# Twenty-four projections turned to 512-column token form, rounded blocks of the norms written from PSUM, and one weight split moved, in a three-block model on one core

## The reference

```python
def sqrelu_mlp(x, w1, w2):
    return jnp.square(jax.nn.relu(x @ w1)) @ w2
...
        x = layer_norm(ALPHA * x + mix, ln1_g[i], ln1_b[i])
        x = layer_norm(ALPHA * x + sqrelu_mlp(x, mlp_w1[i], mlp_w2[i]), ln2_g[i], ln2_b[i])
```

```python
    proj = jnp.einsum("bld,dp->blp", x, w_in)
    qkv, z, a, b, uv, gate_dn, gate_sgu = jnp.split(proj, offsets, axis=-1)
    qkv = jax.nn.silu(causal_depthwise_conv(qkv, conv_w)).astype(f32)
...
    y_dn = jnp.einsum("blc,cd->bld", o.reshape(bsz, seq, DN_DIM).astype(x.dtype), w_dn_out)
    y_sgu = spatial_gating(uv, sgu_ln_g, sgu_ln_b, spatial_w, spatial_b, w_sgu_out)
    y = jax.nn.sigmoid(gate_dn) * y_dn + jax.nn.sigmoid(gate_sgu) * y_sgu
    return jnp.einsum("bld,de->ble", y, w_out)
```

## Time and profile before

| | |
|---|---|
| median of 3 runs | 1267.28 us |
| profiled execution, its own time | 1265.15 us |
| its span | 1263.4 us |
| TensorE busy (matmul) | 1239.5 us, 98% |
| VectorE busy | 806.1 us, 64% |
| ScalarE busy | 607.2 us, 48% |
| mean granted TensorE clock | 0.999 of full speed |
| bytes moved | 205.00 MB, 162 GB/s |

### The profile page before, as it was taken

One profiled execution on the slowest core, in us unless ns is written; L12 is line 12 of the kernel. 1 busy time (PEld: TensorE's weight loads), 2 busy tenths in 40 slices (PEclk: granted clock), 3 DMA queues, 4 the chain that ended last, 5 costly groups with the idle time before them and its releaser, 6 DMA issues.

```text
span 1263.4 us, 20462 instructions
## 1 busy us (share of the span) xinstructions
PE 1239.5 (98%) x8838; PEld 1154.6 (91%) x8838; DVE 806.1 (64%) x946; ACT 607.2 (48%) x702; POOL 164.3 (13%) x137
## 2 busy tenths in 40 slices
PE   8999999999999999999999999999999999999997
PEld 8978999998999899999889999999998999999996
DVE  6477855657655875565888338833777775555556
ACT  4565434345636534434476457645734633333332
POOL 8400400001400040000401300040000050000000
PEclk9999999999999999999999999999999999999999
DMA  9814665553742475557665335672754465555550
GB/s 264 194 34 133 198 236 178 189 200 103 231 151 84 165 237 197 176 192 163 138 138 130 101 101 134 133 102 68 250 190 144 167 216 184 185 183 195 175 197 34
DMA packets 148219, 205.00 MB, mean 162 GB/s; under 512 B 13603, under 2 KB 117778, under 8 KB 148130
## 3 DMA queue, kind: packets, MB, share of 16 engines
q1 hardware_dynamic: 145906, 195.80, 52.1%
q0 software_dynamic: 2224, 7.90, 2.0%
HBM read 202.63 MB, written 1.05 MB: 161 GB/s over the span
## 4 chain that ended last, share of the span: by engine, by line
PE 83%; DVE 7%; DMA 4%; ACT 3%; SPq 2%; issue 1%; DVEq 0%; ACTq 0%
PE PS L385 37%; PE PS L390 18%; PE PS L513 8%; PE PS L456 2%; DMA ring<-in_w_in 2%; DVE w_lo L1158 2%; PE PS L993 2%; PE PS L1006 1%; ACT w_hi L1753 1%; PE PS L394 1%; SPq L2327 1%; PE PS L395 1%; PE PS L396 1%; DMA ring<-in_a_w_out 1%; PE PS L919 1%
## 5 line engine op out<-in xcount | busy, mean ns | idle before, releaser
L1158 DVE TENSOR_TENSOR w_lo<-ring,w_hi 128x2048 fp32r<-128x2048 f32 x182 | 429.9, 2367 | 208.0 <-ACT w_hi L1753 208.0
L1753 ACT ACTIVATE w_hi<-ring 128x2048 fp32r<-128x2048 f32 x182 | 347.7, 1912 | 246.8 <-PE PS L390 225.3
L385 PE MATMUL PS<-x_hi,w_hi 128*128 128x256 f32 x1168 | 284.1, 284 | 0.2 <-DVE x_lo L1650 0.2
L385 PE MATMUL PS<-x_lo,w_hi 128*128 128x256 f32 x1168 | 283.5, 283 | 0.0
L385 PEld LDWEIGHTS PS<-x_hi,w_hi 128*128 128x128 f32 x1168 | 223.7, 192 | 3.3 <-issue 1.5
L385 PEld LDWEIGHTS PS<-x_lo,w_hi 128*128 128x128 f32 x1168 | 224.0, 192 | 1.7
L1765 ACT ACTIVATE AR<-PS 128x512 f32<-128x512 f32 x154 | 87.2, 598 | 271.0 <-PE PS L390 176.9
L390 PE MATMUL PS<-x_hi,w_lo 128*128 128x256 f32 x1184 | 154.4, 283 | 0.2 <-DVE w_lo L1283 0.2
L385 PE MATMUL PS<-w_hi,o_hi 128*128 128x512 f32 x384 | 150.2, 391 | 0.8 <-DVE o_lo L1407 0.8
L385 PE MATMUL PS<-w_hi,o_lo 128*128 128x512 f32 x384 | 150.0, 391 | 0.0
L390 PEld LDWEIGHTS PS<-x_hi,w_lo 128*128 128x128 f32 x1184 | 147.5, 192 | 0.4 <-DVE w_lo L1283 0.4
(11 more groups left out here) (408 smaller groups left out, 1816.1 us busy)
## 6 DMA issues: line engine op xcount, KB each, us to landing
ring<-in_mlp_w SPq DMA_DIRECT2D x64, 1024.0 KB, 5.2
ring<-in_w_in SPq DMA_DIRECT2D x32, 1024.0 KB, 8.5
ring<-in_expert_w_gate SPq DMA_DIRECT2D x16, 1024.0 KB, 5.4
ring<-in_expert_w_up SPq DMA_DIRECT2D x16, 1024.0 KB, 5.4
ring<-in_expert_w_down SPq DMA_DIRECT2D x16, 1024.0 KB, 5.0
ring<-in_c_w_in SPq DMA_DIRECT2D x12, 1024.0 KB, 5.3
ring<-in_a_w_in SPq DMA_DIRECT2D x4, 1024.0 KB, 8.6
ring<-in_c_w_out SPq DMA_DIRECT2D x4, 1024.0 KB, 4.9
```

The source lines that it names most:

```text
L385: mm(out, a, b, start=first and i == 0, stop=False, skip_group_check=True)
L1158: v.tensor_tensor(w_lo[:, m % PARTS], ring[:, index[split[m]] % RING], w_hi[:, m % PARTS].bitcast(F32), ALU.subtract)\
L1753: a(w_hi[:, m % PARTS], ring[:, index[split[m]] % RING], ACT.Copy).then_inc(S("hi_split"), 1)
```

## The change

It has four parts.

**Token pairs.** 24 chunks go in 12 pairs through a new generator `token_pair`: `gv` 2 and 3, `gd` 0 to 3, `gs` 0 to 3, `uv` 6 and 7, `uv` 0 to 3, `yd` 0 to 3 and `yg` 0 to 3. Tokens are stationary and 512 weight columns move, 48 matmuls a pair. The chunks are loaded by `paired`. The second chunk's second half closes the banks: bank j at three quarters and at the end of the pair. Gates and outputs are now held by token, with the evacuations' shapes changed to fit. An `advance` portion is one or two matmuls in turn, so a pair has 32 portions as before.

**The sum of the mixer.** As it is now by token, `y` is transposed by TensorE (`y_turned`, 16 transposes of 128 columns), rounded by ScalarE to `o_hi` and subtracted by VectorE to `o_lo`, from PSUM. VectorE's own rounding of `y` goes. Two `y_turned` stand in the last `yg` pair, two behind the first `sout` chunk.

**Norms.** Except for half (0,1), ScalarE writes its two blocks rounded to `x_hi` straight from PSUM (`direct_half`), and writes them to `n_v` later from the same bank (`plain_half`); VectorE rounds its own two blocks. TensorE waits for the two kinds apart, and does high(1,1) ahead of low(1,0).

**One split.** In the first half of the delta rule VectorE calls `split_ahead` between `convolve(0)` and `convolve(1)`.

```diff
@@ -251,7 +251,8 @@
...
         cols("gk", cwi, 512, 2)
-        cols("gv", cwi, 1024 + W, 3, 1)
+        cols("gv", cwi, 1024 + W, 1, 1)
+        paired("gv", cwi, 1024 + 2 * W, 2, 2)
         cols("gr", cwi, 2048, 4)
...
                 paired("gs", wi, UV + 3072, 4)
-                cols("uv", wi, UV + 1024 + W, 3, 5)
-        cols("uv", wi, UV, 4)
-        cols("yd", A["w_dn_out_2"][0], 0, 4)
-        cols("yg", A["w_sgu_out_2"][0], 0, 4)
+                cols("uv", wi, UV + 1024 + W, 1, 5)
+                paired("uv", wi, UV + 1024 + 2 * W, 2, 6)
+        paired("uv", wi, UV, 4)
+        paired("yd", A["w_dn_out_2"][0], 0, 4)
+        paired("yg", A["w_sgu_out_2"][0], 0, 4)
         rowsof("sout", A["w_out_2"][0], 0, 4)
...
@@ -469,8 +471,14 @@
...
                 def high(m, b):
-                    pe.wait_ge(S("x_hi"), 4 * l + 2 * m + b + 1)
+                    direct = (m, b) != (0, 1)
+                    if direct:
+                        pe.wait_ge(S("x_hi_direct"), 3 * l + 2 * m + b + (m == 0))
+                    else:
+                        pe.wait_ge(S("x_hi"), l + 1)
                     for k in range(4 * b, 4 * b + 4):
+                        if direct and k == 4 * b + 2:
+                            pe.wait_ge(S("x_hi_vector"), 3 * l + 2 * m + b + (m == 0))
                         for i, w in enumerate((wh, wl)):
...
@@ -488,8 +496,8 @@
...
                 high(1, 0)
+                high(1, 1)
                 low(1, 0)
-                high(1, 1)
                 close(low(1, 1), chunk, chunk)
...
+            def token_pair(pre, i, banks, a_hi=x_hi, a_lo=x_lo, ready=None):
+
+                names, ps, issued = ((pre, i), (pre, i + 1)), [None, None], 0
+                for half in range(2):
+                    n = take_high(names[half])
+                    wh, wl = (w[:, n, :].rearrange("p (k n) -> p k n", k=KT // 2) for w in (w_hi, w_lo))
+                    for j in range(2):
+                        if half == 0:
+                            ps[j] = claim(pe, names[j], banks[j])
+                        c = slice(j * P, (j + 1) * P)
+                        for low in range(2):
+                            if low and j == 0:
+                                take_low(names[half])
+                            for k in range(KT // 2):
+                                if (low, j) == (0, 0) and k % 2 == 0 and ready is not None:
+                                    read_out(pe, ready[(KT // 2 * half + k) // 2])
+                                last = low == 1 and k == KT // 2 - 1
+                                for h, a_ in enumerate((a_hi,) if low else (a_hi, a_lo)):
+                                    ins = mm(ps[j], a_[:, KT // 2 * half + k, c], (wl if low else wh)[:, k, :],
+                                             start=(half, low, k, h) == (0, 0, 0, 0), stop=half == 1 and last, skip_group_check=True)
+                                    issued += 1
+                                    if last:
+                                        if half:
+                                            close(ins, names[j], names[1] if j else None)
+                                            filled.append(names[j])
+                                        elif j:
+                                            spent(ins, names[0])
+                                    if issued % 3 != 1:
+                                        yield
+
             def in_turn(work):
-                for i, (chunk, token) in enumerate(work):
-                    if not token:
-                        if chunk[1] % 2 == 0:
-                            yield from pair(*chunk, (6, 7))
-                    else:
-                        yield from triples(chunk, 6 + i % 2, token)
+                for how, *what in work:
+                    yield from how(*what)
...
                 close(ins, ("gb", t))
-            for i in range(1, 4):
-                by_token(("gv", i))
+            by_token(("gv", 1))
+            advance(token_pair("gv", 2, (nxt(), nxt())))
             pe.wait_ge(S("gla_scaled"), 1)
...
                 if hb == 0:
-                    fill = in_turn([(("z", i), False) for i in range(4)] + [(("gd", i), False) for i in range(4)])
+                    fill = in_turn([(pair, "z", i, (6, 7)) for i in (0, 2)] + [(token_pair, "gd", i, (6, 7)) for i in (0, 2)])
                 else:
-                    fill = in_turn([(("gs", i), False) for i in range(4)] + [(("uv", i), True) for i in range(5, 8)])
+                    fill = in_turn([(token_pair, "gs", i, (6, 7)) for i in (0, 2)] + [(triples, ("uv", 5), 6, True), (token_pair, "uv", 6, (7, 6))])
                 advance(fill, 6)
...
-            steps = triples(("uv", 0), 1, True)
+            steps = token_pair("uv", 0, (1, 0))
             advance(steps, 8)
...
                 norm_sums("dn", 1, j, 2, "dn_squares", 2 + j)
-            turn[0] += 2
             advance(steps)
-            for i in (1, 2, 3):
-                by_token(("uv", i))
+            advance(token_pair("uv", 2, (4, 5)))
             pe.wait_ge(S("o_split"), TT + 2 + 4 + 4)
-            for i in range(2):
-                by_feature(("yd", i), o_hi, o_lo)
+            advance(token_pair("yd", 0, (6, 7), o_hi, o_lo))
             pe.wait_ge(S("sp_w_masked"), 1)
             for j in range(2):
-                ps = claim(pe, ("uw", j), nxt())
+                ps = claim(pe, ("uw", j), 2 + j)
                 for g in range(4):
...
                 close(ins, ("uw", j))
-            by_feature(("yd", 2), o_hi, o_lo)
+            steps = token_pair("yd", 2, (1, 0), o_hi, o_lo)
+            advance(steps, 8)
             for j in range(2):
...
                 for j in range(2):
-                    ps = claim(pe, ("sp", t, j), nxt())
+                    ps = claim(pe, ("sp", t, j), 4 + 2 * t + j)
                     for g in range(4):
...
                     close(ins, ("sp", t, j))
-            by_feature(("yd", 3), o_hi, o_lo)
+            advance(steps)
             for t in range(TT):
...
             transposes(u_u, "gT")
-            by_feature(("yg", 0), ready=[("gT", j) for j in range(4)])
-            for i in (1, 2, 3):
-                by_feature(("yg", i))
+
+            def y_turned(i):
+
+                pe.wait_ge(S("y_rows"), i + 1)
+                ps = claim(pe, ("yT", i), 4 + i % 2)
+                for b in range(4):
+                    ins = nc.tensor.transpose(ps[:, b * P:(b + 1) * P], flat(s_y[:, 2 * i:2 * i + 2])[:, b * P:(b + 1) * P], ident[:])
+                close(ins, ("yT", i))
+
+            advance(token_pair("yg", 0, (2, 3), ready=[("gT", j) for j in range(4)]))
+            steps = token_pair("yg", 2, (6, 7))
+            advance(steps, 12)
             for i in range(2):
-                pe.wait_ge(S("o_split"), TT + 2 + 4 + 4 + i + 1)
-                by_rows(("sout", i), 2 * i, "m4", i == 0)
+                y_turned(i)
+            advance(steps)
+            pe.wait_ge(S("o_split"), TT + 2 + 4 + 4 + 2)
+            by_rows(("sout", 0), 0, "m4", True)
+            for i in (2, 3):
+                y_turned(i)
+            by_rows(("sout", 1), 2, "m4", False)
             steps = last_rows([("sout", 2), ("sout", 3)], 4, "m4", [("o_split", TT + 2 + 4 + 4 + 3), ("o_split", TT + 2 + 4 + 4 + 4)], 4, ("eg", 0))
...
@@ -1200,17 +1246,25 @@
...
-                ve.wait_ge(S("x_hi"), 4 * l + 2 * t + b + 1)
+                if (t, b) != (0, 1):
+                    ve.wait_ge(S("x_hi_vector"), 3 * l + 2 * t + b + (t == 0))
+                    read_out(ve, (f"nT{l}", t, b, 0))
+                else:
+                    ve.wait_ge(S("x_hi"), l + 1)
                 ks, ts = slice(4 * b, 4 * b + 4), slice(t * P, (t + 1) * P)
...
                 ps = bank((f"nT{l}", t, b, 1), 0 if t else 1)
+                ks, ts = slice(4 * b + 2, 4 * b + 4), slice(t * P, (t + 1) * P)
                 for i in range(2):
                     k = 4 * b + 2 + i
-                    ins = v.tensor_scalar(n_v[:, k, t * P:(t + 1) * P], ps[:, i * P:(i + 1) * P], col(f"g{l}", k), col(f"b{l}", k), ALU.mult, ALU.add)
+                    ins = v.tensor_scalar(n_v[:, k, ts], ps[:, i * P:(i + 1) * P], col(f"g{l}", k), col(f"b{l}", k), ALU.mult, ALU.add)
                 evacuated(ins, (f"nT{l}", t, b, 1))
+                if (t, b) != (0, 1):
+                    read_out(ve, (f"nT{l}", t, b, 1))
+                    v.tensor_copy(x_hi[:, ks, ts], n_v[:, ks, ts]).then_inc(S("x_hi_vector"), 1)
...
                     convolve(n)
+                    if (hb, n) == (0, 0):
+                        split_ahead(pieces_for["gc"], 2)
...
                 read(("yg", i))
-                after(v.tensor_tensor(y, y, sg, ALU.add))
-                split_operand(y, 2 * i)
+                v.tensor_tensor(y, y, sg, ALU.add).then_inc(S("y_rows"), 1)
+                if i % 2:
+                    for j in (i - 1, i):
```

(65 more changed lines are left out.)

## The result

Over 8 runs each: before 1266.16 us (1265.62 to 1268.05), changed kernel 1259.79 us (1258.28 to 1263.77), ratio 0.9949 [0.9940, 0.9958] (in brackets, here and below, the 95% interval), so 6.4 us faster. Forecast was 1259.7. The profiled execution took 1259.07 us with a span of 1257.3, 6.1 less than before.

What follows compares the result with a forecast made beforehand. TensorE, busy 1239.5 of 1263.4 us, was taken to bound the kernel. Pairs -6.7, transposes +1.9, portions +0.3, norms -1.8 and split -1.3 gave -7.6, from 1267.28 to 1259.7 us; range 1254.5 to 1264.5.

Steps and rivals of the forecast that it cites:

- Token pairs, -6.7: Projections: one 512-column matmul costs 11.7 ns less than two of 256, 0.56 us a pair, 12 pairs give 6.7 us.
- 512 costs twice 256: Rival on the token pairs: 512 columns cost as much as twice 256, nothing saved there, 1266.4 us; 6%.
- the 2.5 ns of the Trainium skill: Token pairs: fixed cost about 2.5 ns a matmul, so 1.4 us saved instead of 6.7, estimated 1265.0; no chance given.
- TensorE starved: Rival: late splits make TensorE wait for w_lo inside pairs, 1.3 us each, 1275.3 us; 7%.
- Transposes, +1.9, no wait: Mixer's sum: 16 new transposes on TensorE add 1.9 us, bounds 1.7 and 2.2, with no wait taken.
- Portions, +0.3: Delta rule's chain: shorter portions bring TensorE earlier to points needing other engines; 0.3 us given back, bounds 0 and 1.5.
- Norms, -1.8: Five norms: TensorE's wait turns from x_hi to x_lo, 0.5 us less each, 1.8 in sum after D moves later.
- D: Start of ScalarE's deviation in a norm's second tile, the forecast's counting point; expected 0.33 us later at norm 1.
- + 0.05 + 0.69, then four matmuls: Norm's end: plain_half(1,1), VectorE's last x_lo, four matmuls of 0.48, 0.05 between engines, reaching D + 6.1.
- Moved split, -1.3: Delta rule's first half: the 1.87 us wait for w_lo goes, kk is late next; 1.3 us gained, bounds 0 and 2.1.
- towards 1.3: Sign of being right: the 1.87 us gap near 650 gone and TensorE's wait at kk grown towards 1.3 us.

Runs made afterwards that it cites:

- e3: The changed kernel with every 512-column matmul of the token pairs issued as two of 256 columns; 1266.91 us, ratio 1.0001 against before.
- e1: The kernel before with the moved split alone; 1265.65 us, ratio 0.9996 against before.
- e6: The kernel before with GpSimd's last add behind norm 3 held until VectorE's small gates instruction is issued, plus the moved split; ratio 0.9974.
- e5: The kernel before with GpSimd's last add behind norm 3 held until VectorE's small gates instruction (L1477) is issued; ratio 0.9985.
- e4: The changed kernel with gd, gs, yd and yg by feature as before, 4 of 12 pairs left, no transposes of y; 1261.92 us, ratio 0.9967.
- e2: The kernel before with the norms' part alone; 1266.04 us, ratio 0.9999 against before.
- e7: The changed kernel with VectorE's small gates instruction made to wait for GpSimd's last add, forcing the order of before; ratio 0.9965 against before.

## Why the prediction was right, and where it was right by luck

**The time.** 1259.7 and 1259.79 agree better than the account behind them. I counted -7.6 from 1267.28, the median of three runs; over eight it is 1266.16, and the change brought 6.4 (6.1 in the profile). These 1.1 us are luck. The stretches of the first table add up like this:

| | forecast | profile |
|---|---|---|
| pairs, transposes, portions | -4.5 | -4.6 |
| norms | -1.8 | -0.9 |
| first half of the heads to `kk` | -1.3 | -2.6 |
| 2nd MLP | 0 | +1.2 |
| before norm 0 | 0 | +0.7 |
| sum | -7.6 | -6.1 |

**Token pairs, -6.7.** Right: 6.6 by e3's runs, 6.0 by its profile. TensorE's busy time fell by 3.4, where I had about 5. The rivals "512 costs twice 256" and the 2.5 ns of the Trainium skill ("TensorE: Matmul & The Clock Gate", "Wait — 56ns, not 53.3ns?") are out: by the latter e3 was to lose an estimated 1.4. No wait for `w_lo` appeared inside a pair, so "TensorE starved" is out too.

**Transposes, +1.9, no wait.** Right: two records of 1.03 and 1.04, +1.8 when doubled.

**Portions, +0.3.** Too small: about 0.9, within the bounds of 0 and 1.5. The 252 merged matmuls in the chain gave 1.18 + 0.83 = 2.0 us where 11.7 ns each make 2.9. With the old count, in e3, both stretches are as before (127.82, 74.07). Of the 0.9, 0.2 is what I described: at the second `kk` VectorE's scalings end at 798.61, and TensorE starts at 798.67, 0.45 behind its last start, where 0.23 is usual. The rest stays open. It is luck that the three terms together are right: the merges outside the chain (4.0 in place of 3.8) and the new form (0.3) made up for it.

**Norms, -1.8.** Mechanism right, size off: 1.1 (0.9 in this pair of profiles, as norm 3 of before stood alone). TensorE's waits moved from `x_hi` to `x_lo` as written. At norm 1, ScalarE's, VectorE's and TensorE's rows from D = 306.46:

```profile
309.83 1.51 ACT L1846 ACTIVATE AR<-PS,vec 128x128 f32<-128x128 f32 x4
```
```profile
310.43 0.29 DVE L1267 CAST x_hi<-AR 128x256 fp32r<-128x256 f32 x1
310.75 1.39 DVE L1255 TENSOR_TENSOR x_lo<-AR,x_hi 128x512 fp32r<-128x512 f32 x2
```
```profile
311.50 1.44 PE L489 MATMUL PS<-w_hi,x_lo 128*128 128x256 f32 x8
312.77 0.28 PE L387 MATMUL PS<-x_hi,w_hi 128*128 128x256 f32 x1
```

ScalarE's last block ends at D + 4.88 (forecast 4.84), so that step held. The step that was mis-sized is the end, "+ 0.05 + 0.69, then four matmuls". VectorE's last `x_lo` starts 0.10 behind ScalarE's end, not 0.05, and ends at 312.14, D + 5.68 in place of D + 5.58; the same 0.10 stands at all five norms. TensorE's four matmuls begin 0.05 behind it, as forecast, but take 0.58, not 0.48, as the first of them stands 0.23 apart from the next; TensorE goes on at D + 6.31, not D + 6.1. Against D + 6.62 a norm gains 0.31, not 0.5. D was later by 0.17 at norm 1, not 0.33. Norm 3 gained nothing.

**Moved split, -1.3.** This step failed in mechanism. I wrote that the wait at `kk` would grow "towards 1.3"; alone (e1) it grew to 1.85 and the split brought 0.5, in the changed kernel it vanished and the stretch gave 2.56. What I didn't see in the profile of before was the 2.13 us of VectorE's L1477 beside GpSimd's L2217. With that order fixed the split is worth 1.1 by the stretch (1.4 by the runs, e6 against e5), and the order itself 1.4 (1.9 by the runs, e5). That the changed kernel got the good order without being told to is luck.

**What I had not in the sum.** The 2nd MLP's +1.20 is a late weight transfer. ScalarE's row for the first chunk of norm 3, before and after:

```profile
598.06 1.92 ACT L1753 ACTIVATE w_hi<-ring 128x2048 fp32r<-128x2048 f32 x1 [0.33 <-DMA ring<-in_w_in]
```
```profile
598.79 1.91 ACT L1817 ACTIVATE w_hi<-ring 128x2048 fp32r<-128x2048 f32 x1 [1.78 <-DMA ring<-in_w_in]
```

VectorE's `w_lo` and the sums of the norm wait behind it, and TensorE 1.03 at L685. In all six profiled kernels without pairs this wait is 0.3 to 0.7, in all eight with pairs (e4's four among them) 1.6 to 2.3. The norms' part and the moved split are in kernels of both kinds, and e4 has no transposes of y, so it goes with the pairs; not with the count of matmuls, as e3 has it too. The chunk is the same 1 MB in both kernels; it lands 13.6 us after its issue before and 15.0 after (13.6 to 14.0 in the six, 14.8 to 15.6 in the eight). Why stays open; it wasn't tried.

The +0.70 before norm 0 is no effect of the change: this stretch took 116.7 to 120.1 us over the fourteen profiled executions, kernels with and without each part among both the short and the long. In these two executions 0.6 of it is one wait for a `w_hi` in the first 14 us (0.4 before, 1.0 after). Together the two took back 1.9, where the flipped order had given 1.3 more than forecast.

## What to carry to other kernels

When an engine's tiny instruction shows microseconds of duration, look at what GpSimd does at that moment: a stall can be inside the record and not in the idle time before it, and no list of waits names it. Test the parts of a change alone before crediting them; here the split and the order of two engines were worth 0.8 and 1.4 alone and 2.6 together, by the stretch that holds them. Where a change has several small terms, time the same stretch in every kernel: the medians of the runs could not tell most of these terms apart. A wait of TensorE that is "only" 2 us is to be priced with the clock that may fall behind it.

## What the hardware showed that I had not expected

How much the turns of VectorE and GpSimd cost: GpSimd's 128x1024 operation lasted 2.39 us beside an idle VectorE and 4.29 to 4.34 (once 4.45) beside splits, VectorE's split 2.28 and 4.50, and the order of two starts 0.01 us apart fell either way. VectorE's operation with one tensor operand in SBUF was held up too (L1481 in e5, 2.34 in place of 0.17). Its copies out of PSUM beside the same operation were not: 0.41, and 0.19 with GpSimd busy (before) as with GpSimd idle (e5). The granted clock read 0.54 to 0.61 in two stretches of 2 us behind waits of 2.15 (e2) and 1.85 (e7), and not behind waits of 1.87 (before) and 1.85 (e1).
